# Splitting sixteen 8 KB SBUF buffers as four for weights and seven for gathered rows, instead of three and eight

## The chip, the cores and the metric

The kernel runs on one core of a Trainium2 chip. The metric is the device time of one execution in microseconds. The kernel before took 2333.25 us (median of 3 runs, 2330.32 to 2334.89). Below, a "piece" is a block of weights that one DMA brings into SBUF, a "row" is one gather of the last stage, and an "add" is the step that uses up a row.

## The reference, cut to what matters

One step of a one-layer streaming encoder, in float32, for 512 prompt frames and 32 frames of a second stream that has a cache of 512 past frames.

```
h = RMSNorm(x);  z = h @ w_in                 # q, k, v of two attentions, forget logits, gates
oA = DiffAttn(...), oB = FoX(...)             # 8 heads each
x = x + (sigmoid(gA)*(oA@w_pa) + sigmoid(gB)*(oB@w_pb)) @ w_o
q = RMSNorm(x) @ peer_wq                      # 1024 -> 2048
per frame and head: top 16 of 128 + 128 subkeys -> 16 experts of 16384
act = gelu(u[e] . x);  x = x + sum(softmax weight * act * v[e])   # 8 heads * 16 experts
y = RMSNorm(x)
```

For each frame 128 experts are fetched from a table whose line holds u (1024 floats) and v (1024 floats) of one expert, so 8 KB.

## The kernel before, in words

The 544 frames are five tiles: t = 0 to 3 of 128 frames, t = 4 of 32. A tile's work has two parts. Its *front* is attention (16 heads' steps, here called attend), norms and turns, the output projections, the product-key scores and the top-16 search (here called route). Its *experts* are 128 slots; slot s fetches, for each of the 128 frames (one per partition), the 8 KB line of that frame's expert. That is one row: a GpSimd indirect DMA of 1 MB (`gather`, line 677). For t = 4 each of the 32 frames takes four partitions, so there are 32 slots. In all 4 x 128 + 32 = 544 rows.

A row passes through three steps: VectorE takes the dot product of its u half with the frames (`dot`, L1618), ScalarE applies gelu to the 128 dot products (L941), and the v half is added, weighted. The add is done either by TensorE with a diagonal matrix (`add_v`, L1293, two matmuls of 512 columns) or by VectorE (L1643); a fixed table `ADDERS` says which. Slots are handled in pairs (HALF = 2), called half-blocks: both dots, then both weights or VectorE adds. TensorE runs the adds of a pair one step late, after the front piece that follows the pair (`held`, in the plan loop of TensorE).

All engines follow one list, `PLAN`, written by `make_plan`. It begins with the projection of tile 0 (27 chunks of w_in on 128 frames), then tile 0's front with the first chunks of the projection of tiles 1 to 4 between, and then, for t = 0 to 3, the pairs of experts of tile t with the front of tile t + 1 spread between them. For t = 0 the remaining projection chunks come first. The experts of t = 4 stand alone at the end. Each engine takes its part of the list in order, so a pair's dots wait behind the front piece ahead of them and the other way round.

Weights come in 159 pieces in the order of `WEIGHTS`: 52 chunks of w_in and 2 small ones, and for each front 4 of w_pa (1 MB), 4 of w_pb (0.5 MB), 4 of w_o, 8 of peer_wq and one of subkeys (1 MB each). w_pa and w_pb alternate. SyncE loads piece n into buffer n % WBUFS as soon as TensorE has finished piece n - WBUFS (`w_used`, raised at lines 1059, 1218, 1227, 1238, 1263, 1273):

```
if n >= WBUFS:
    sp.wait_ge(w_used, n - WBUFS + 1)
...
sp.dma_start(wb[:, 0:src.shape[1]], src).then_inc(landed, 16)
```

In the same queue stand the loads of q for the next tile, the saves of k and v, and the cache loads for the last tile.

Rows use slot s % RING. GpSimd issues row s when row s - RING has been dotted and added (line 677 in `gather`):

```
if s >= RING:
    who, count = ADDERS[s - RING]
    waits = [(dotted, s - RING + 1), (adders[who], count)]
gather(k, a, s % RING, waits)
```

Before the first row is fetched, the memory of the row buffers holds the inputs, h, and the front area of tile 0 (12,000 columns of each partition at most, of 16,384 with eight rows and 14,336 with seven).

Of the kernel before, what the change touches and what calls it, by code (L numbers as in the profile page):

```python
# [50 lines left out]
N_KEYS = 128  # L51
PC = 16
CW = 256
WBUFS = 3
RING = 8
BLOCK = 4
HALF = BLOCK // 2
DIAGS = 9
# [169 lines left out]
def landed_counts():  # L228

    count, out = [0] * WBUFS, []  # L230
    for n, _ in enumerate(WEIGHTS):
        count[n % WBUFS] += 16
        out.append(count[n % WBUFS])
    return out
# [112 lines left out]
def build(nc, d):  # L347
    with ExitStack() as ctx:  # L348
        def sb(name, shape, dt=F32):
            return ctx.enter_context(nc.sbuf_tensor(name, shape, dt))  # L350

        def sem(name):
            return ctx.enter_context(nc.semaphore(name))
# [4 lines left out]

        ring_all = sb("ring", [P, RING * 2 * D])
        ring = ring_all[:, :].rearrange("p (r n) -> p r n", r=RING)  # L360
        qT = sb("qT", [P, 12 * P])
# [3 lines left out]
        vb = sb("vb", [P, TILES, HEADS * DVB])  # L365
        wbuf = sb("wbuf", [P, WBUFS, KT, CW])
        bias = sb("bias", [P, HEADS, 2 * P])
# [21 lines left out]
        gw = sb("gw", [P, 2, SLOTS])  # L389
        dots = sb("dots", [P, RING])  # L390
        gel = sb("gel", [P, RING])
        gelw = sb("gelw", [P, RING])
        diag = sb("diag", [P, DIAGS, P])
# [47 lines left out]

        w_landed = [sem(f"w_landed{i}") for i in range(WBUFS)]
        w_used = sem("w_used")
# [65 lines left out]
        slot_free = sem("slot_free")  # L509
        row_landed = [sem(f"row_landed{r}") for r in range(RING)]  # L510
        seeded = sem("seeded")
# [82 lines left out]
        def _(sp):  # L594
# [11 lines left out]
            def save_kv():  # L606
                sp.wait_ge(z_stored, UNITS[len(GROUPS) - 1, CHUNKS])
                sp.dma_start(d["o_kaT"].rearrange("(k p) n -> p k n", p=P), kaT[:, :, :]).then_inc(kv_saved, 16)
                sp.dma_start(d["o_kbT"].rearrange("(k p) n -> p k n", p=P), kbT[:, :, :]).then_inc(kv_saved, 16)
                sp.dma_start(d["o_va"][0:SEQ, :].rearrange("(k p) n -> p k n", p=P), va[:, 0:4, :]).then_inc(kv_saved, 16)  # L610
                sp.dma_start(d["o_va"][SEQ:NTOK, :], va[0:DEC, 4, :]).then_inc(kv_saved, 16)
                sp.dma_start(d["o_vb"][0:SEQ, :].rearrange("(k p) n -> p k n", p=P), vb[:, 0:4, :]).then_inc(kv_saved, 16)
                sp.dma_start(d["o_vb"][SEQ:NTOK, :], vb[0:DEC, 4, :]).then_inc(kv_saved, 16)
# [12 lines left out]
            for n, (kind, piece) in enumerate(WEIGHTS):  # L626
                if n == last_z + 1:
                    save_kv()
                if n == WBUFS:
                    sp.dma_start(va[64:96, TILES - 1, :], d["norm2_g"].broadcast_to([32, D])).then_inc(rows_landed, 16)  # L630
# [1123 lines left out]
```

## Time and profile before

| | |
|---|---|
| median of 3 runs | 2333.25 us |
| profiled execution, device time | 2327.74 us |
| its span, first to last instruction | 2325.6 us |
| PE (matmul) busy | 1798.4 us, 77% |
| DVE busy | 1508.2 us, 65% |
| POOL busy | 757.1 us, 33% |
| ACT busy | 592.7 us, 25% |
| bytes moved by DMA | 765.01 MB, mean 329 GB/s |
| queue of the rows (q0) / of weights and SyncE (q1) | 570.46 MB / 169.48 MB |
| mean granted TensorE clock | 0.902 |

The span is the time between the first and the last instruction; the device time of the same execution is 2.1 us longer. PE, PEld, DVE, ACT and POOL are TensorE's matmuls, TensorE's weight loads, VectorE, ScalarE and GpSimd. "SPq" is SyncE's queue of DMA issues. Each group in the views of waits says for which instruction an engine stood idle and what ended the idle time.

### The profile page before, as it was taken

How to read it: one execution, taken by the hardware profiler on the slowest of the kernel's cores; microseconds unless marked ns; L12 is line 12 of the kernel's file. 1: busy time of each engine (PE TensorE's matmuls, PEld its weight loads, DVE VectorE, ACT ScalarE, POOL GpSimd, SP SyncE). 2: the span in 40 equal slices, each digit the busy share in tenths (PEclk: the TensorE clock that was granted, in tenths of full speed). 3: DMA queues.
4: the chain of work that ended last, by engine and by line, in shares of the span. 5: the costliest groups of instructions: out<-in, count | busy, mean ns of one | idle time of the engine just before them, and what ended most of it. 6: DMA issues, size and time to landing. Idle time of an engine off the chain costs nothing. (4 is left out here: it accounts for less than half of the span.)

```text
span 2325.6 us, 22972 instructions
## 1 busy us (share of the span) xinstructions
PE 1798.4 (77%) x7392; PEld 1085.4 (47%) x7392; DVE 1508.2 (65%) x3478; ACT 592.7 (25%) x1631; POOL 757.1 (33%) x697
## 2 busy tenths in 40 slices
PE   7988898789967776778787677878656787787755
PEld 6855774346635562334663233456422343563211
DVE  0021109576676459778667977785678788659966
ACT  3232011211143112344012234411222343013211
POOL 0000000454432023434334433342436344335443
PEclk9998999899997898888899889989998889999878
DMA  7832654999797787889999988899999879999987
GB/s 250 306 134 68 219 195 135 396 381 397 291 406 287 290 348 274 316 308 355 421 421 420 369 346 310 308 409 421 419 411 381 318 299 344 416 421 391 357 320 303
DMA packets 132071, 765.01 MB, mean 329 GB/s; under 512 B 19056, under 2 KB 34080, under 8 KB 44272
## 3 DMA queue, kind: packets, MB, share of 16 engines
q0 software_dynamic: 78336, 570.46, 61.8%
q1 hardware_dynamic: 30688, 169.48, 19.4%
q10 hardware_dynamic: 22928, 23.61, 2.9%
q8 instruction: 59, 0.97, 0.2%
q14 instruction: 60, 0.49, 0.1%
HBM read 744.77 MB, written 18.30 MB: 328 GB/s over the span
## 5 line engine op out<-in xcount | busy, mean ns | idle before, releaser
L677 POOL DMA_INDIRECT ring<-in_uv,stage x544 | 695.0, 1278 | 1122.8 <-PE acc L1293 452.8
L1293 PE MATMUL acc<-ring,diag 128*128 128x512 f32 (+1 forms) x1268 | 682.1, 687 | 225.3 <-ACT diag L953 133.0
L1618 DVE CUSTOM_DVE_ANT_0 ring<-ring,xb 128x1024 f32<-128x1024 f32 x544 | 646.1, 1220 | 115.1 <-DMA ring<-in_uv,stage 95.3
L1293 PEld LDWEIGHTS acc<-ring,diag 128*128 128x128 f32 (+1 forms) x1268 | 255.5, 213 | 604.6 <-issue 281.3
L941 ACT ACTIVATE gel<-dots 128x1 f32<-128x1 f32 x544 | 100.4, 199 | 880.7 <-DVE dots L1618 879.8
L1643 DVE SCALAR_TENSOR_TENSOR vsum<-ring,coefd,vsum 128x1024 f32<-128x1024 f32 x222 | 285.7, 1287 | 8.1 <-DVE coefd L1636 0.2
L1055 PE MATMUL pz<-F,wbuf 128*128 128x416 f32 (+1 forms) x656 | 244.4, 533 | 34.6 <-ACT F L814 29.8
L1055 PEld LDWEIGHTS pz<-F,wbuf 128*128 128x128 f32 (+1 forms) x656 | 127.1, 196 | 148.0 <-issue 148.0
L697 POOL COPY stage<-idx 128x4 int32<-128x4 int32 x136 | 59.3, 436 | 417.2 <-DVE gw L1574 399.0
L1636 DVE TENSOR_SCALAR coefd<-gel,gw 128x1 f32<-128x1 f32 x227 | 47.5, 209 | 160.8 <-ACT gel L941 160.4
L941 ACT ACT_TABLE_LOAD x67 | 86.0, 1283 | 36.8 <-issue 22.7
L1629 DVE TENSOR_SCALAR diag<-ident,gel,gw 128x128 f32<-128x128 f32 x159 | 55.1, 356 | 59.9 <-ACT gel L941 57.7
L1140 PE MATMUL pt<-ident,F 128*128 128x128 f32 (+2 forms) x224 | 35.1, 275 | 66.7 <-DVE F L1459 56.9
L1055 PE MATMUL pz<-wbuf,F 128*128 128x256 f32 (+1 forms) x384 | 85.0, 381 | 1.9 <-PE pz L1055 1.9
L1055 PE MATMUL pz<-ring,wbuf 128*128 128x128 f32 (+1 forms) x656 | 79.6, 281 | 6.8 <-ACT ring L778 3.4
L1055 PEld LDWEIGHTS pz<-ring,wbuf 128*128 128x128 f32 (+1 forms) x656 | 75.1, 191 | 14.0 <-issue 13.1
L1259 PE MATMUL pz<-F,wbuf 128*128 128x128 f32 x512 | 65.9, 291 | 15.5 <-DMA wbuf<-in_w_q 14.0
L1055 PEld LDWEIGHTS pz<-wbuf,F 128*128 128x128 f32 (+1 forms) x384 | 64.4, 170 | 22.7 <-issue 6.8
L1259 PEld LDWEIGHTS pz<-F,wbuf 128*128 128x128 f32 x512 | 63.1, 205 | 18.3 <-DMA wbuf<-in_w_q 15.7
L1259 PE MATMUL ps<-F,wbuf 128*128 128x128 f32 x512 | 62.5, 282 | 9.5 <-DMA wbuf<-in_w_q 7.7
L1259 PEld LDWEIGHTS ps<-F,wbuf 128*128 128x128 f32 x512 | 60.3, 197 | 13.5 <-DMA wbuf<-in_w_q 8.8
L1140 PEld LDWEIGHTS pt<-ident,F 128*128 128x128 f32 (+2 forms) x224 | 22.4, 143 | 90.8 <-DVE F L1459 72.2
(299 smaller groups left out, 2090.4 us busy)
## 6 DMA issues: line engine op xcount, KB each, us to landing
wbuf<-in_w_z SPq DMA_DIRECT2D x52, 1024.0 KB, 6.1
wbuf<-in_w_q SPq DMA_DIRECT2D x40, 1024.0 KB, 10.5
wbuf<-in_w_pa SPq DMA_DIRECT2D x20, 1024.0 KB, 10.8
wbuf<-in_w_o SPq DMA_DIRECT2D x20, 1024.0 KB, 10.0
wbuf<-in_w_pb SPq DMA_DIRECT2D x20, 512.0 KB, 9.2
ring<-in_uv,stage POOLq DMA_INDIRECT x544, 10.1
zt_mid<-F ACTq DMA_DIRECT2D x28, 192.0 KB, 5.1
wbuf<-in_w_sk SPq DMA_DIRECT2D x5, 1024.0 KB, 10.4
```

Source lines behind the costliest of these rows:

```text
L677: pool.indirect_dma_start(out=ring[:, slot, :], out_offset=None, in_=d["uv"], in_offset=bass.IndirectOffsetOnAxis(ap=stage[:, a, k:k + 1], ...
L697: nc.gpsimd.tensor_copy(stage[:, a, :], idx[:, t % 2, BLOCK * b:BLOCK * b + BLOCK]).then_inc(staged[a], 1)
L941: nc.scalar.activation(gel[:, slot:slot + 1], dots[:, slot:slot + 1], ACT.Gelu).then_inc(gelued, 1)
L1055: last = nc.tensor.matmul(out, left, right, start=(k == 0), stop=(k == KT - 1))
L1140: last = nc.tensor.transpose(pt[0:w, j * nq:(j + 1) * nq], p[0:nq, j * P:j * P + w], ident[0:nq, 0:nq])
L1259: last = nc.tensor.matmul(banks(t)[f % 4][:, 0:streamed(t)], w[:, k, j * P:(j + 1) * P], fa(t).xbT[:, k, 0:streamed(t)], start=(k == 0), s ...
L1293: last = nc.tensor.matmul(acc[0:nq, c * 512:(c + 1) * 512], diag[:, parity, 0:nq], ring[:, slot, D + c * 512:D + (c + 1) * 512], start=Fal ...
L1618: nc.vector.tensor_tensor_reduce(out=u, in0=u, in1=xb[:, t % 2, :], scale=1.0, scalar=0.0, op0=ALU.mult, op1=ALU.add, accum_out=dots[:, sl ...
L1629: nc.vector.tensor_scalar(diag[:, parity, 0:nq], pick[:, 0:nq], gel[:, slot:slot + 1], g, ALU.mult, ALU.mult).then_inc(coef_set, 1)
L1636: nc.vector.tensor_scalar(c, gel[:, slot:slot + 1], g, None, ALU.mult).then_inc(coefd_set, 1)
L1643: last = nc.vector.scalar_tensor_tensor(vsum[:, :], v, c, vsum[:, :], ALU.mult, ALU.add)
```

## The change

Two constants are changed. Everything that is derived from them follows: the buffer that a piece or a row uses, the piece or row that each issue waits for, the number of semaphores, and the place at which two small norm loads stand in SyncE's queue (after piece 4 and not piece 3).

```
-WBUFS = 3
-RING = 8
+WBUFS = 4
+RING = 7
```

One buffer for a piece is 8 KB of each partition, as is one for a row, so the SBUF in use stays the same but for three columns of small per-slot arrays.

## Rows read from the trace of the kernel before

**Rows 1.** The page, part 2: GB/s moved in 40 slices of 58.1 us.
```profile
GB/s 250 306 134 68 219 195 135 396 381 397 291 406 287 290 348 274 316 308 355 421 421 420 369 346 310 308 409 421 419 411 381 318 299 344 416 421 391 357 320 303
```

**Rows 2.** Busy time of each engine in stretches; last: granted clock, DMA share, GB/s.
```profile
core 0: us, PE busy (x) PEld busy (x) DVE busy (x) ACT busy (x) POOL busy (x), PEclk, DMA share, GB/s
743.00:801.00 58.00, 44.34 (x255) 39.88 (x256) 24.51 (x55) 1.98 (x9) 7.49 (x8) 0.87 0.89 359
801.00:855.00 54.00, 45.37 (x311) 39.13 (x309) 20.75 (x38) 12.00 (x32) 12.65 (x10) 0.91 0.80 322
945.00:1090.00 145.00, 111.86 (x379) 58.69 (x378) 111.91 (x233) 64.69 (x138) 55.85 (x56) 0.88 0.85 328
1118.00:1172.00 54.00, 40.35 (x227) 35.45 (x226) 35.88 (x72) 2.23 (x11) 15.51 (x15) 0.87 1.01 421
1653.00:1735.00 82.00, 47.66 (x97) 18.51 (x96) 57.58 (x215) 19.26 (x73) 30.64 (x30) 0.96 1.02 418
2033.00:2096.00 63.00, 51.76 (x324) 40.73 (x324) 35.86 (x64) 11.09 (x40) 21.59 (x19) 0.92 1.00 415
2096.00:2150.00 54.00, 42.30 (x94) 17.33 (x92) 53.36 (x200) 18.81 (x74) 29.94 (x28) 0.97 0.98 396
2224.00:2312.00 88.00, 49.65 (x80) 8.84 (x80) 62.53 (x115) 8.27 (x35) 41.38 (x39) 0.81 0.95 388
```

**Rows 3.** Waits in 743 to 860 us: engine, line, releaser, us in total, times, longest.
```profile
PE ps L1234 <- DMA wbuf<-in_w_o: 3.7, 1, 3.7
PE pz L1223 <- DMA wbuf<-in_w_pb: 3.1, 1, 3.1
PE pz L1214 <- DMA wbuf<-in_w_pa: 2.7, 1, 2.7
PE pz L1259 <- DMA wbuf<-in_w_q: 2.5, 1, 2.5
PE ps L1214 <- DMA wbuf<-in_w_pa: 1.5, 1, 1.5
PE ps L1259 <- DMA wbuf<-in_w_q: 0.7, 1, 0.7
```

**Rows 4.** The weight buffers over the whole span: idle us and times until a landing.
```profile
  DMA wbuf<-in_w_q: 46.2, 30
  DMA wbuf<-in_w_pa: 38.6, 17
  DMA wbuf<-in_w_o: 34.1, 18
  DMA wbuf<-in_w_pb: 23.2, 15
  DMA wbuf<-in_w_sk: 5.5, 4
```

**Rows 5.** Waits of VectorE for a row: 1090 to 1290, 1515 to 1735, 2224 to 2326 us.
```profile
DVE ring L1618 <- DMA ring<-in_uv,stage: 16.0, 11, 2.9
...
DVE ring L1618 <- DMA ring<-in_uv,stage: 35.0, 18, 3.7
...
DVE ring L1618 <- DMA ring<-in_uv,stage: 23.6, 22, 2.9
```

**Rows 6.** The timeline around row 161 (1047.94 its issue, 1059.36 its dot): start, us.
```profile
1047.94 2.00 POOL L677 DMA_INDIRECT ring<-in_uv,stage  x1 [0.30 <-issue]
1053.74 0.93 POOL L677 DMA_INDIRECT ring<-in_uv,stage  x1 [3.81 <-issue]
1059.36 1.22 DVE L1618 CUSTOM_DVE_ANT_0 ring<-ring,xb 128x1024 f32<-128x1024 f32 x1
```

**Rows 7.** Rows' time from issue to landing, 945 to 1090 us.
```profile
DMA to landing us min/median/max: 5.6/8.4/13.2
```

**Rows 8.** DMA issues 1118 to 1232 us: KB each, median us to landing.
```profile
wbuf<-in_w_q SPq DMA_DIRECT2D x8, 1024.0 KB, 11.4
ring<-in_uv,stage POOLq DMA_INDIRECT x28, 22.8
```

## The prediction

> **What bounds the kernel now.** I began with the page's slices of moved bytes [rows 1]. They stand at 409 to 421 GB/s in three blocks (slices 20 to 22, 27 to 30, 35 and 36) and lower elsewhere; no slice is above 421, so I take that as what this core's DMA gives. 1 MB (a row or a piece) then costs 1.048 / 421 = 2.5 us of DMA. The engines' busy time in stretches comes next [rows 2]. It tells four kinds of stretch apart: the weight part of a front with the DMA nearly but not quite full (743 to 855 us: share 0.89 and 0.80); the same part in later tiles with the DMA full (1118 to 1172 us: 1.01, 421 GB/s; 2033 to 2096 us: 1.00); attend, where no resource is full (945 to 1090 us: DMA 0.85, DVE 111.9 of 145 us); and the rows of the last tile, where the DMA is full again (2224 to 2312 us: 0.95 with its start). Then the waits. In the weight part of the first of these fronts TensorE waits for pieces, six waits of 14.2 us together [rows 3]. Over the whole span the weight buffers show 147.6 us of such waits [rows 4], but that view counts the weight load and its matmul, so about half, 74 us, is time. VectorE waits for rows 16.0, 35.0 and 23.6 us in the stretches with a full DMA [rows 5]; in the attend stretches the view of waits has none. So the bound changes: bytes in the full stretches, a chain across TensorE, VectorE and ScalarE in the others, with late pieces of weights in one of them.
>
> **The change part by part.** No instruction, no DMA and no byte is added or removed. Only the moment changes at which 159 pieces and 544 rows are issued.
>
> *Pieces, front of tile 1 (743 to 855 us).* The fourth buffer does two things. A fourth piece (the second of w_pb) is already there when the front begins, and a fourth of w_q is fetched while TensorE waits for the norm and the turn. The first removes the wait of 3.1 us on w_pb, the second those of 2.5 and 0.7 us on w_q [rows 3], 6.3 us in all. The three between (2.7, 1.5 and 3.7 us, 7.9 us) are waits on pieces in steady flow, with the DMA at 0.89: one more piece in flight brings them forward only as far as there is room. I take a third, 2.6 us. Sum 8.9 us off. Lower end 3.1 us (the first wait alone), upper end 14.2 us. TensorE sets the pace here (busy 44.3 of 58 and 45.4 of 54 us, VectorE 24.5 and 20.8 [rows 2]), and VectorE waits for no row, so what TensorE saves should be kept through the route stage.
>
> *Pieces, fronts of tiles 2 to 4.* What is left of the 74 us, about 60 us of waits, lies here. The DMA is full from before the weight part to well after it (421, 418 and 415 GB/s [rows 2]), and the engines work down one list in which pairs of rows and pieces alternate. In such a stretch the time to reach a point in the list is the bytes up to that point over 421 GB/s; a piece that comes sooner makes a row come later. I take 0 for tiles 2 and 3. In tile 4's front the rows are ahead of their dots, and VectorE is at its limit just behind (53.4 of 54 us at 2096 to 2150), so pieces that come sooner can start that stage sooner, until the DMA binds: of its 54 us it had 2% left, of the 63 before none. I take 2 us off. Ends for all three: 0, and 20 us each if the waits were plain stalls.
>
> A row shows how the two queues share a full DMA: between 1118 and 1232 us a row takes 22.8 us from issue to landing and a piece of w_q 11.4 us [rows 8], so a deep queue of rows does not hold the pieces back in proportion. The Trainium skill, "DMA: Bandwidth & Descriptors", section "Queues, rings and completion order", says that each DMA engine takes turns between the queues that have work, a packet at a time. By that rule a piece more in flight would not raise the weights' share while both queues have work, and the steady-flow third above (2.6 us) would be 0; by rows 3 I keep it.
>
> *Pieces, elsewhere.* In the first projection (0 to 135 us) and the first front (240 to 355 us) no wait for a piece over 0.5 us is in the view of waits, so 0; the front end could only lose if the fourth piece, issued at the start, crowded the small loads, and it stands behind them in the same queue. The copies and cache loads in SyncE's queue are each issued one piece sooner, behind waits of their own: 0.
>
> *Rows, attend stretches (945 to 1090, 1365 to 1515, 1800 to 1955 us).* With eight buffers row s waits for the add of row s - 8; for an odd s that is the odd row four pairs back. With seven it is the even row three pairs back: the odd row of each pair is issued about one pair later, the even row (released by the odd add just before it) as before. Row 161 shows the size [rows 6]. It was issued at 1047.94 us and dotted at 1059.36. Its new releaser is the add that now releases row 162, issued at 1053.74. So it goes from 11.4 us ahead to 5.6 us ahead, and the shortest landing in this stretch is 5.6 us, the median 8.4 [rows 7]. That row is just in time if it goes out into an empty DMA, which the later issue makes likelier (share 0.85), and 2.8 us late at the median. I read it as one of the tightest. VectorE has 33 us of idle time in these 145, so a late dot is partly absorbed. I take 1 us per stretch, 3 us on. Lower end 0; upper end: a quarter of the 68 pairs late by 2.8 us, 48 us.
>
> *Rows, entry to a full stretch and end of a tile.* Where the DMA becomes full (1100, 1515, 1965 us, and the last pairs of a tile), one row less has been fetched ahead, 2.5 us of DMA. There are three entries and three tile ends, 6 x 2.5 = 15 us if each time the DMA stood idle for want of that row. Between the attend share of 0.85 and the full 1.00 it was partly idle [rows 2], so I take a third, 5 us on. Lower end 0, upper 15.
>
> *Rows, last tile.* VectorE waits 22 times for a row there, 23.6 us [rows 5]: the bytes bind it (32 rows x 2.5 = 80 of 88 us). With one row less the queue is shorter but not empty: 0, upper end 5 us.
>
> **Sum.** 2325.6 - 8.9 - 2 + 3 + 5 = 2322.7 us of span, 2324.8 us with the 2.1 us around it. The profiled execution was 5.5 us under the median of the runs, so 2330.3 us there: 3 us or 0.12% faster, which is within what a measurement of this kernel can tell from no change (0.2%, 4.7 us).
>
> **The rivals.**
> 1. *The weight waits are worth more.* Then the first front gives all of its 14.2 us, and in tile 4 the fourth piece of w_q, fetched during the norm and the turn, starts the route stage sooner by the 2 x 2.5 = 5 us that a piece takes when it alternates with a row. 2333.25 - 14.2 - 5 + 5 = about 2319 us. For it: about 60 us of waits in later fronts, and in the last of these a VectorE at its limit just behind. Against it: DMA at 1.00 in all of them. It should show as fronts of tiles 2 to 4 that shorten while GB/s stays at 421.
> 2. *Seven rows are too few (slower).* The mechanism is the odd row of a pair in attend. VectorE does the dots in order, so a late odd row holds its add, the add holds the row three pairs on, and the loop closes over three pairs and not four. It decides once adds come later than (three pairs' time - landing of 8.4 us) after their dots. With 145 us for some 22 pairs (45 rows issued), 6.6 us each, that is 19.8 - 8.4 = 11.4 us, and an add by TensorE comes one step late: a pair's 6.6 us and its own pair's dots, gelu and diagonals behind the dot, so not far from it. If a third of the upper end (16 us) comes true and the entries cost 5, the time is 2333.25 - 8.9 - 2 + 16 + 5 = about 2343 us. For it: rows 6. Against it: VectorE waits for no row in attend now, so there is cover to lose first.
> 3. *The change does next to nothing*, for the fronts' gain stays with the first wait (3.1 us) and the rows lose nothing: 2330 us. It can't be told from the forecast by time, and counts with it.
>
> **How the numbers follow.** Forecast (with rival 3): 0.42; rival 1: 0.30; rival 2: 0.28. Forecast's own range 2326 to 2336 us. Of its 0.42, about 0.04 lies below the bound of 0.2% and 0.02 above it. So faster 0.34, same 0.36, slower 0.30. The range that holds 8 in 10 reaches into both rivals: 2318 to 2347 us.
>
> **What would show each step.** Right: no wait of TensorE on w_pb in the front of tile 1 and the q pieces without a wait; that front shorter by 6 to 12 us; at 421 GB/s the full stretches as long as before within 3 us; in attend a few waits of VectorE for rows, each under 3 us, together under 10 us. Wrong: fronts of tiles 2 to 4 shorter by 5 us or more each (rival 1), or waits for rows in attend of over 15 us with attend stretches longer than 145 to 155 us (rival 2). The prediction as a whole fails if the last row's dot comes over 5 us away from where it was, with tiles' spans not shifted as said.

## The result and the profile after

The changed kernel took 2338.55 us (median of 20 runs, 2331.03 to 2349.48) and the kernel before, run beside it, 2328.07 us (20 runs, 2319.63 to 2341.2). The ratio is 1.0045, interval 1.0031 to 1.0058: 10.5 us slower. The forecast was 0.12% faster; the time lies inside the range of 2318 to 2347 us, on the side that I had given 0.30. The profiled execution has a span of 2336.3 us, 10.7 us more than that of before, at a granted clock of 0.895 (before 0.902).

The page of the changed kernel: its span and part 2, GB/s in slices of 58.4 us. These answer to [rows 1]: still no slice above 421, and the three blocks near it are again slices 20 to 22, 27 to 30 and 35 and 36, the last two a little lower (391 to 421, and 414).

```profile
span 2336.3 us, 22973 instructions
...
GB/s 267 291 146 66 218 195 138 390 374 393 281 396 289 344 358 261 311 319 378 421 420 404 355 333 314 311 421 391 418 398 391 296 302 336 414 414 387 337 320 304
```

The table of stretches of the changed kernel answers to [rows 2], same columns (granted clock, DMA share and GB/s last). The stretches are chosen by eye for about the same work (TensorE's matmuls of the first two are 571 in the changed kernel, 566 in [rows 2]; the one at 2033 us holds 344 against 324 and is longer by that), so they show rates and not what was gained.

```profile
743.00:793.00 50.00, 40.72 (x247) 36.32 (x246) 22.68 (x51) 2.37 (x8) 10.33 (x10) 0.88 1.01 415
793.00:845.00 52.00, 45.84 (x324) 39.82 (x323) 23.65 (x44) 12.40 (x34) 10.84 (x10) 0.93 0.83 334
938.00:1083.00 145.00, 112.48 (x375) 58.75 (x376) 110.44 (x231) 64.49 (x137) 54.74 (x53) 0.87 0.83 321
1110.00:1164.00 54.00, 38.38 (x224) 33.78 (x223) 37.55 (x74) 2.43 (x12) 14.86 (x15) 0.84 1.01 421
...
1653.00:1735.00 82.00, 53.09 (x100) 20.46 (x99) 56.66 (x212) 19.36 (x73) 29.65 (x29) 0.90 1.02 418
2033.00:2099.00 66.00, 54.58 (x344) 41.05 (x342) 36.69 (x65) 11.42 (x41) 21.66 (x20) 0.95 1.01 418
2099.00:2156.00 57.00, 43.10 (x88) 17.31 (x88) 51.53 (x190) 18.20 (x72) 30.82 (x28) 0.94 0.97 382
2235.00:2323.00 88.00, 49.84 (x80) 8.98 (x80) 62.37 (x115) 8.38 (x35) 38.45 (x39) 0.81 0.94 388
```

The weight part of the first front is shorter, and its DMA went from 0.89 to 1.01 in the first half. The full stretches are full as before. Attend is unchanged (VectorE 110.4 of 145 us, before 111.9).

TensorE's waits for pieces in the first front, the changed kernel at 743 to 850 us, against the six of [rows 3] (engine, instruction, releaser, us in total, times, longest):

```profile
PE ps L1234 <- DMA wbuf<-in_w_o: 2.8, 1, 2.8
...
PE pz L1214 <- DMA wbuf<-in_w_pa: 1.1, 1, 1.1
...
PE pz L1234 <- DMA wbuf<-in_w_o: 0.7, 1, 0.7
```

14.2 us became 4.6. The waits on w_pb and on w_q are gone. Over the whole span the idle time in front of the weight buffers (us, times), against the 147.6 us of [rows 4], is 62.2 us:

```profile
  DMA wbuf<-in_w_pa: 33.7, 15
...
  DMA wbuf<-in_w_o: 13.4, 10
  DMA wbuf<-in_w_q: 9.6, 11
...
  DMA wbuf<-in_w_sk: 5.5, 4
```

What the weights gained, the rows lost. VectorE's waits for rows, the changed kernel at 938 to 1083, 1083 to 1285, 1513 to 1735 and 2235 to 2336 us, against none, 16.0, 35.0 and 23.6 us in [rows 5]. The first of them is not attend's: it is the wait of row 127's dot, the last of tile 0, which starts at 937.08 us and runs into the window.

```profile
DVE ring L1618 <- DMA ring<-in_uv,stage: 1.6, 1, 1.6
...
DVE ring L1618 <- DMA ring<-in_uv,stage: 39.4, 23, 3.8
...
DVE ring L1618 <- DMA ring<-in_uv,stage: 58.0, 32, 3.7
...
DVE ring L1618 <- DMA ring<-in_uv,stage: 23.6, 22, 2.5
```

The same over the whole span, from part 5 of the page (busy us, mean ns of one, idle before, its main releaser), first before, then after:

```profile
L1618 DVE CUSTOM_DVE_ANT_0 ring<-ring,xb 128x1024 f32<-128x1024 f32 x544 | 646.1, 1220 | 115.1 <-DMA ring<-in_uv,stage 95.3
```

```profile
L1618 DVE CUSTOM_DVE_ANT_0 ring<-ring,xb 128x1024 f32<-128x1024 f32 x544 | 649.1, 1221 | 188.6 <-DMA ring<-in_uv,stage 168.5
```

So 85 us less idle in front of weights (load and matmul both counted) and 73 us more in front of rows, while the time changed by 10 us. Neither figure by itself is time on the path: most waits were swapped for others.

Row 161, the row of [rows 6], in the changed kernel's timeline (start, duration, engine): issue, then dot.

```profile
1046.58 0.94 POOL L677 DMA_INDIRECT ring<-in_uv,stage  x1 [5.13 <-issue]
...
1052.19 1.22 DVE L1618 CUSTOM_DVE_ANT_0 ring<-ring,xb 128x1024 f32<-128x1024 f32 x1
```

It is issued 5.6 us ahead of its dot, as worked out, lands 0.1 us ahead of it, and no wait stands at the dot. Landing times in this stretch (938 to 1083 us) against [rows 7], and the issues at 1110 to 1220 us (KB each, median us to landing) against [rows 8]:

```profile
DMA to landing us min/median/max: 5.4/7.8/11.9
```

```profile
wbuf<-in_w_q SPq DMA_DIRECT2D x8, 1024.0 KB, 11.6
ring<-in_uv,stage POOLq DMA_INDIRECT x28, 21.4
```

A row now waits 21.4 us and not 22.8 in the full stretch, as there is one less of them; a piece takes 11.6 us, before 11.4.

**Where the time is.** To compare kernels I measured, in each timeline, from the start of one row's dot to that of another. Rows are numbered 0 to 543 over all tiles, so each stage holds the same work in every kernel. Two profiles of each of the first three kernels are given, since single stages differ by up to 3.4 us between two executions of the kernel before.

| stage (first to last row's dot), us | before | 3 and 7 buffers | 4 and 7 (changed) | 3 and 6 |
|---|---|---|---|---|
| weights of front 1 (82 to 100) | 118.4, 115.0 | 113.8, 114.2 | 107.9, 107.7 | 113.7 |
| weights of fronts 2 to 4 (178 to 206, 306 to 334, 438 to 464), sum | 348.6, 348.0 | 349.6, 350.8 | 346.4, 344.5 | 353.0 |
| route, tiles 1 to 3 (206 to 246, 334 to 374, 464 to 502), sum | 349.5, 352.5 | 355.5, 355.9 | 356.6, 354.1 | 380.2 |
| ends of tiles, the last ten rows and what follows up to attend (118 to 136, 246 to 264, 374 to 392, 502 to 512), sum | 204.3, 201.1 | 215.0, 217.0 | 215.7, 211.7 | 225.1 |
| attend (136 to 170, 264 to 298, 392 to 430), sum | 341.1, 340.2 | 338.6, 340.2 | 339.8, 338.5 | 353.4 |
| turn after attend (170 to 178, 298 to 306, 430 to 438), sum | 60.1, 60.1 | 64.3, 64.1 | 66.2, 66.2 | 69.4 |
| last tile (512 to 543) | 80.0, 80.2 | 79.8, 79.9 | 79.5, 79.8 | 81.9 |

Means against before: ends +11.0, turns +6.1, routes +4.4, attend -1.5, weights of fronts 2 to 4 -2.8, of front 1 -8.9. Sum +8.3 us, of the 10.5 timed. The spans of these profiles differ by 12.2 us in the mean, and 3.5 of that lies ahead of row 82, where executions scatter most: that row's dot starts at 727.2 and 725.1 us in before and at 728.1 and 731.2 us in the changed kernel, and the wait for rows is not longer there by more than 2 us.

### The profile page after: what moved, and what is told of

Read it like the earlier page. It is cut to its first block and busy times, and to the rows that moved or that the text cites. A ratio compares the mean times of both kernels' runs of the same rounds, so it can differ in the third digit from the quotient of the medians.

```text
span 2336.3 us, 22973 instructions
## 1 busy us (share of the span) xinstructions
PE 1805.9 (77%) x7392; PEld 1083.4 (46%) x7392; DVE 1510.6 (65%) x3478; ACT 593.7 (25%) x1631; POOL 738.8 (32%) x697
## 5 line engine op out<-in xcount | busy, mean ns | idle before, releaser
L677 POOL DMA_INDIRECT ring<-in_uv,stage x544 | 675.7, 1242 | 1150.6 <-issue 362.0
L1293 PE MATMUL acc<-ring,diag 128*128 128x512 f32 (+1 forms) x1268 | 698.7, 701 | 239.9 <-ACT diag L953 139.1
L1293 PEld LDWEIGHTS acc<-ring,diag 128*128 128x128 f32 (+1 forms) x1268 | 261.9, 218 | 629.6 <-issue 290.1
L941 ACT ACT_TABLE_LOAD x67 | 86.0, 1283 | 36.7 <-issue 22.7
L1259 PE MATMUL pz<-F,wbuf 128*128 128x128 f32 x512 | 61.0, 278 | 6.2 <-DMA wbuf<-in_w_q 2.9
L1259 PEld LDWEIGHTS pz<-F,wbuf 128*128 128x128 f32 x512 | 58.4, 192 | 8.9 <-issue 5.0
## 6 DMA issues: line engine op xcount, KB each, us to landing
wbuf<-in_w_q SPq DMA_DIRECT2D x40, 1024.0 KB, 10.7
wbuf<-in_w_o SPq DMA_DIRECT2D x20, 1024.0 KB, 14.7
```

Of the source, the lines that this page charges most:

```text
L677: pool.indirect_dma_start(out=ring[:, slot, :], out_offset=None, in_=d["uv"], in_offset=bass.IndirectOffsetOnAxis(ap=stage[:, a, k:k + 1], ...
L941: nc.scalar.activation(gel[:, slot:slot + 1], dots[:, slot:slot + 1], ACT.Gelu).then_inc(gelued, 1)
L1259: last = nc.tensor.matmul(banks(t)[f % 4][:, 0:streamed(t)], w[:, k, j * P:(j + 1) * P], fa(t).xbT[:, k, 0:streamed(t)], start=(k == 0), s ...
L1293: last = nc.tensor.matmul(acc[0:nq, c * 512:(c + 1) * 512], diag[:, parity, 0:nq], ring[:, slot, D + c * 512:D + (c + 1) * 512], start=Fal ...
```

## The experiments

**One part alone: seven rows, three pieces**, and **one row fewer still**.

```
-RING = 8
+RING = 7        (second kernel: RING = 6)
```

> Three buffers for pieces as before, seven row buffers: the row part of the change alone. Theory A (the trace after: the loss is one row less fetched ahead where the DMA is full and at the ends of the tiles, 20 us, and the pieces give 10 us back): about 18 to 22 us slower than before, ratio 1.008 to 1.010; waits of VectorE for rows well over the 95 us of before; attend stretches as long as before. Rival B (the fourth piece takes DMA from the rows, and seven rows alone cost little): within 5 us of before.

> Three buffers for pieces, six row buffers. If what is lost is bytes fetched ahead (one row, 2.5 us, at some eight places), six rows lose about twice what seven lose: some 40 us, ratio 1.017. If it is the loop of an odd row that closes over three pairs where it closed over four, six rows close over three pairs too, for both rows of a pair, and lose little more than seven: 20 to 28 us, ratio 1.009 to 1.012.

Measured: 2348.52 us with seven rows (before 2328.63), ratio 1.0086, interval 1.0069 to 1.0103, so +20 us, as theory A had it. With six 2407.59 us, ratio 1.0335, interval 1.0317 to 1.0353: +79 us, where neither theory had over 40. VectorE's line for the dots in part 5, first seven rows, then six:

```profile
L1618 DVE CUSTOM_DVE_ANT_0 ring<-ring,xb 128x1024 f32<-128x1024 f32 x544 | 648.4, 1220 | 156.5 <-DMA ring<-in_uv,stage 137.1
```

```profile
L1618 DVE CUSTOM_DVE_ANT_0 ring<-ring,xb 128x1024 f32<-128x1024 f32 x544 | 652.1, 1221 | 249.3 <-DMA ring<-in_uv,stage 231.8
```

The first buffer taken away costs 20 us and the second 59 us more. In the table above the ends (+13.3, then +22.4 us) and the turns (+4.1, +9.3) go about in proportion to the number of rows missing. Routes (+4.7, +29) and attend (-1.3, +12.7) don't: the second row costs there many times what the first did. (Numbers are means over the profiles of a kernel, where there are two.) VectorE's waits for rows lie in the same places: in the ends 8.8 and 8.5 us in the two profiles of before, 18.9 and 20.8 with seven rows, 31.0 with six; in the routes 32.9 and 33.1, then 40.9 and 40.6, then 68.3; in attend 0, then 1.0 and 1.2, then 28.7. This points to two mechanisms, of which the second is hardly paid for at seven rows. That it is the loop from a row's add to the landing of the row six on is my reading; no run shows it by itself, and with six rows there is one profile.

**Are the full stretches bound by bytes?** The first three pieces of the next front (pa, pb, pa: 2.5 MB) are fetched in the route stage, when the DMA is full, and lie unused through attend. One wait in SyncE's queue keeps them back for fronts 2 to 4 until all rows of the tile before are added (`summed`), which falls into the stretch called an end here. It is done to both kernels.

```
 if n >= WBUFS:
     sp.wait_ge(w_used, n - WBUFS + 1)
+if (kind, piece) == ("pa", 0) and fronts >= 2:
+    sp.wait_ge(summed, fronts - 1)
```

> The kernel before (3 and 8) with one wait more in SyncE's queue: the first pieces of the next front are not fetched behind the subkeys but only once the tile before is summed, for the fronts of tiles 2, 3 and 4. That takes 2.5 MB, 6.2 us of DMA, out of each of the full stretches and puts it into attend, where the DMA has room. If bytes bind those stretches, as I said: 8 to 18 us faster, ratio 0.992 to 0.997. If the rows' latency or VectorE binds the route stage there, 0 to 4 us.

> The changed kernel (4 and 7) with the same wait. The pieces held back are four, 3.5 MB or 8.7 us of DMA each time. If bytes bind: 12 to 22 us faster than the changed kernel, so 2 to 12 us faster than before. If the rows' latency binds since there are seven buffers, it stays within 5 us of the changed kernel (ratio to before 1.002 to 1.006).

Measured: the kernel before with the wait 2316.21 us, ratio 0.9941 (0.9918 to 0.9964), 13.7 us faster by the ratio; the changed kernel with it 2324.4 us, ratio to before 0.9987 (0.9969 to 1.0005), so 0.58% or 13.5 us under the changed kernel. (There four pieces are held back, pa, pb, pa, pb, which is 3 MB or 7.5 us and not the 3.5 MB or 8.7 us of the expectation.) SyncE's timeline of the first, around the place (the pieces after w_sk went out from 1220.55 us on in the kernel before):

```profile
1217.37 0.33 SPq L640 DMA_DIRECT2D wbuf<-in_w_sk  x1
...
1365.65 0.33 SPq L640 DMA_DIRECT2D wbuf<-in_w_pa  x1
1366.02 0.43 SPq L640 DMA_DIRECT2D wbuf<-in_w_pb  x1
```

And its windows at two tile ends (columns as in [rows 2]), to be held against the ends shown below:

```profile
1333.00:1388.00 55.00, 39.14 (x85) 15.65 (x86) 41.16 (x83) 16.69 (x41) 21.55 (x22) 0.88 1.01 411
1768.00:1823.00 55.00, 34.01 (x64) 12.76 (x64) 41.91 (x81) 9.61 (x25) 27.17 (x26) 0.83 1.01 414
```

The DMA is now at 1.01 in these ends, which carry 2.5 MB more each, and the two together take 113.8 us, in the two profiles of before 113.8 and 110.9. The gain is in the routes of tiles 1 and 2: 113.6 us against 117.2 and 118.0, and 124.0 against 131.7 and 130.5, together 11 us, where 2.5 MB / 421 = 6.2 us each is what the bytes say. In the changed kernel the same two routes lose 6.5 and 6.1 us of the 7.5 by bytes. In tile 0's route, where the DMA was idle for 21 of 81 us before, holding the pieces gives nothing (81.6 us). So the full stretches are bound by bytes, in both kernels, and a piece moved out of one is worth nearly its bytes. The ends of tiles 1 and 2 are not: they took in 2.5 MB more each and were no longer than in before's first profile.

**The pieces' part alone.** Four buffers and eight rows together find no room in SBUF, so this was not tried in that form. Instead a fourth place was made, for pieces of fronts 1 to 4 only, out of the q buffer widened from 1536 to 2048 columns; the 2 KB per partition for it come from DIAGS = 5 in place of 9. It can be used only from the end of a tile's attend on, so unlike the changed kernel's fourth buffer it holds nothing through attend. The core of the edit:

```
-DIAGS = 9
+DIAGS = 5
-qT = sb("qT", [P, 12 * P])
+qT = sb("qT", [P, KT * CW])
...
-if n >= WBUFS:
-    sp.wait_ge(w_used, n - WBUFS + 1)
+if BEFORE[n] >= 0:                        # last piece in the same place
+    sp.wait_ge(w_used, BEFORE[n] + 1)
+if PLACES[n] == WBUFS and BEFORE[n] < last_sk:
+    sp.wait_ge(scored, 24 * (fronts + 1)) # q of this tile has been used
```

> Eight row buffers and three for pieces, and a fourth place for pieces that costs no row buffer: from the end of a tile's attend to its subkeys q lies unused, and its memory (made 512 columns wider; the diagonals of the adds have five buffers and not nine for it) takes every fourth piece in the fronts of tiles 1 to 4. It is the piece part of the change without the row part. If the two parts add up (changed kernel = row part + piece part), it is 8 to 12 us faster than before, ratio 0.995 to 0.997. If the piece part helps only because fewer rows compete, it is within 4 us of before.

Its control, DIAGS = 5 alone:

> The kernel before with five buffers for diagonals where it has nine, the control for the run before this one: within 3 us of before, since an add is at most two pairs behind its diagonal.

Measured: 2312.08 us, ratio 0.9941 (0.992 to 0.9962); the control 2325.03 us, ratio 0.9992 (0.9972 to 1.0012). The pieces' part is then 0.9941 / 0.9992 = 0.9949, 12 us faster. From the other side, the changed kernel over the one with seven rows and three pieces is 1.0045 / 1.0086 = 0.9959, 9.5 us faster. By the intervals the first can be off by some 7 us and the second by 5, so they agree, and both are clear of zero. TensorE's waits for pieces in the first front (738 to 862 us) of the kernel with the part-time buffer, same columns as above:

```profile
PE ps L1262 <- DMA wbuf<-in_w_o: 2.8, 1, 2.8
PE ps L1242 <- DMA wbuf<-in_w_pa: 2.5, 1, 2.5
PE pz L1242 <- DMA wbuf<-in_w_pa: 1.1, 1, 1.1
PE pz L1262 <- DMA wbuf<-in_w_o: 0.6, 1, 0.6
```

**Both things that paid**, the part-time fourth place and the wait, with eight rows:

> Both: the fourth place in q's memory with eight row buffers, and the first pieces of the next front held back until the tile before is summed. The wait alone gave 12 to 14 us; the fourth place should give 8 to 12 more: 2306 to 2312 us where before is at 2329, ratio 0.990 to 0.993. Any less and the two draw on the same time.

Measured: 2306.82 us, ratio 0.9913 (0.9892 to 0.9933), 20 us under the kernel before and the fastest here. The two gains apart, 13.7 us each by their ratios, would add up to 27.5, 7 us more than the 20. Each of the three ratios is uncertain by 5 us, so the 7 us are not clear of noise, and that the two draw on the same time is not shown. The profiles speak against it: from row 82's dot to the end of the span they take 1595.8 us in the mean of before, 1583.8 with the wait, 1577.0 with the place and 1562.8 with both, so there the gains of 12.0 and 18.8 us add up (33.0). What is missing lies ahead, mostly before the first row, where neither edit changes what is issued: that row was issued at 416.6 us with both, at 403.3 and 408.1 in before, 413.6 and 407.1 with one. What made that head longer is open.

**A second profile of three kernels**, to know how far a stage's length can be trusted:

> The kernel before once more, for a second profile of it. What differs between the two profiles of one kernel, stretch by stretch, is the size under which a difference to the changed kernel says nothing: I expect up to 5 us by the start of the rows and in the front of tile 1, under 2 us in each later stretch.

> The changed kernel once more, for a second profile. If the loss sits where the first profile has it, the stretches from the last route pairs of a tile to the third pair of the next are again 3 to 4 us longer than in both profiles of before (55 us at the end of tile 0, 56 at tile 2), the attend stretches are not, and the share of idle DMA grows by what the stretch grows. If the rows are held by a full DMA and not by the seven buffers, the idle DMA stays.

> Three and seven once more, for the same stretches: ends of tiles together 8 to 14 us longer than before with as much more idle DMA, turns 2 to 5 us, attend within 2 us each. The front of tile 1 tells the second thing: 113 to 116 us there (first profile 113.8, before 115.0 and 118.4) would mean that seven rows cost nothing in that front and that the fourth piece alone makes it 108.

Measured, one execution each: before 2320.47 us; changed 2334.21 and seven rows with three pieces 2355.8 us, both beside 2326.56 us for before. The stages are in the table. The second profile of before is 7 us shorter, 3.4 of it in the weights of front 1, and single later stages differ by as much (the end of tile 1 took 58.0 and 54.8 us, the last route 100.6 and 104.0), more than the 2 us that I expected, so a single difference under 3.5 us says nothing. The sums of the ends, of the turns and of the routes are larger with seven rows than with eight in every pair of profiles. One thing expected did not come: in the second profile of the changed kernel the end of tile 0 took 55.2 us, as in before.

## Why the prediction was wrong, step by step

**Pieces, front of tile 1: right in size, with one part of three not shown.** Foretold -8.9 us; the stage is 8.9 us shorter than the mean of before. That the two agree to a tenth is luck: the kernel with the wait and the control, which do here what before does, took 112.7 and 114.2 us, and against the mean of all four the gain is 7.3. The wait on w_pb went, as said, and that on w_q all but 1.1 us in the second profile. Those in steady flow were to give a third of their 7.9 us. In the kernel with the part-time place and eight rows they still add up to 7.0 us (2.8, 2.5, 1.1, 0.6), and in the changed kernel's two profiles they are 4.6 and 7.1. With three pieces they are 7.9 and 7.5 in before, but 6.2 with the wait, 4.2 and 4.6 with seven rows and 4.3 in the control, so no gain on them is shown. Against seven rows and the control the stage shortens by 6.2 us (seven rows; the changed kernel against them) and 6.8 (the control; the part-time place against it), about the 6.3 of the first two parts. The rule of the Trainium skill that was weighed there ("DMA: Bandwidth & Descriptors", "Queues, rings and completion order"), by which this part would be 0, is nearer to these rows than my third.

**Pieces, fronts of tiles 2 to 4: right, the last too small.** Foretold 0, 0 and -2 us. Against seven rows and three pieces, the changed kernel's weight part of front 4 is 4.8 us shorter (112.0 and 112.1 against 116.3 and 117.3), the other two within what repeats differ by (115.3 and 115.9 against 115.9 and 117.1; 119.1 and 116.5 against 117.4 and 116.4). The 60 us of waits there were nearly all time that the DMA needed anyway. With eight rows the same part is 110.7 us with the part-time place, 116.5 and 116.2 in before and 115.0 in the control. Of rival 1 the part in front 4 came true (5 us there), the rest did not: front 1 gave 7 to 9 us and not 14.2. Pieces together: foretold -10.9, measured -9.5 to -12 us.

**Rows, attend: too dear.** Foretold +3 us, measured -1.5, which is within what repeats differ by. In the stretch of [rows 6] no dot of attend waits for a row, and in all three attends together they wait 2.2 and 1.6 us. Rival 2's loop of three pairs, which I had named as the way to be slower, is not what made it slower: attend is no longer with seven rows. It does begin to bind with six (+12.7 us).

**Rows, entry to a full stretch and end of a tile: this step failed.** I had the right mechanism, one row less fetched ahead, with a price of 2.5 us a place, and then took a third of 6 x 2.5 = 15 us because the DMA is "partly idle" between attend and the full stretch. Measured with seven rows alone: four ends +13.3 and three turns +4.1 us, which is 17.4 / 7 = 2.5 us a place, the full price in the mean; and routes, for which I had no term, +4.7. That is 22 us where 5 stood. VectorE's waits for rows grew by about as much there (ends +11.2, turns +4.7, routes +7.8), which ties the loss to rows that land late. Only the mean is 2.5 us: single ends grew by 1.7 to 5.9 us, two of the turns by 0.6 and 0.7 and the third by 2.9, and which places count was settled after the result. The ends of the kernel before (second profile), then with seven rows and three pieces, then changed; tiles 0 to 2, columns as in [rows 2]:

```profile
921.00:976.00 55.00, 38.48 (x89) 16.25 (x89) 40.47 (x81) 19.45 (x43) 20.60 (x21) 0.84 0.79 309
1335.00:1390.00 55.00, 37.45 (x93) 15.24 (x92) 42.49 (x81) 16.21 (x37) 22.71 (x23) 0.91 0.90 365
1770.00:1826.00 56.00, 36.07 (x77) 14.03 (x76) 42.25 (x81) 9.46 (x26) 24.71 (x25) 0.85 0.91 368
```

```profile
923.00:981.00 58.00, 40.74 (x89) 17.12 (x89) 40.47 (x81) 19.45 (x43) 22.41 (x20) 0.82 0.77 292
1343.50:1400.30 56.80, 40.05 (x96) 16.50 (x95) 42.51 (x81) 16.34 (x37) 22.69 (x24) 0.88 0.86 344
1783.00:1846.00 63.00, 39.10 (x78) 15.16 (x77) 42.94 (x81) 9.57 (x28) 25.71 (x25) 0.79 0.85 344
```

```profile
917.00:975.00 58.00, 40.90 (x89) 17.21 (x89) 40.57 (x82) 19.45 (x43) 22.27 (x20) 0.82 0.77 295
1337.00:1396.00 59.00, 43.44 (x96) 17.45 (x94) 42.36 (x80) 16.13 (x37) 22.79 (x23) 0.83 0.85 336
1780.00:1839.00 59.00, 33.33 (x72) 13.02 (x72) 41.81 (x80) 8.82 (x25) 24.00 (x24) 0.84 0.88 361
```

VectorE is busy for the same 40.5 and 42.4 us, to 0.1, in the first two ends of all three. The DMA share falls: in the end of tile 1 from 0.90 to 0.86 and 0.85. Idle DMA, (1.01 - share) times length, summed over the four ends, is 37.1 and 36.7 us in the two profiles of before, 44.8 and 44.1 with seven rows, and 44.0 and 40.5 in the changed kernel. So with seven rows 7.5 of the 13.3 us are idle DMA, and most of the rest is bytes: 68.4 MB came in the ends, against 66.0 in before, which is 5.7 us at 421 GB/s, nearly all of it in the ends of tiles 2 and 3. They had not been fetched ahead. I had read idle DMA as spare room that would hide the loss. It is room for other traffic, as the pieces held back show, but not for rows, which had no free buffer to go to. At the end of a tile the front piece between the pairs is gone, and the last ten dots come 2.0 to 2.1 us apart in the mean in before, faster than the 2.5 us in which the DMA brings a row; in the changed kernel they come 2.2 to 2.5 us apart. What was fetched before lets VectorE run ahead, and the DMA can only fetch ahead into a free buffer. In the route before it the DMA stands idle for want of a free buffer: row 118 of the changed kernel landed at 895.18 us and was dotted at 916.77, so its buffer was taken for 21 us with data that waited. Routes of tiles 1 to 3 have 13 and 16 us of idle DMA in the two profiles of before and 21 in both with seven rows, worked out in the same way. One buffer fewer is one row fewer in store.

The end of tile 0 shows it row by row. The kernel before: dot of row 118, issue of row 125, dot of row 125.

```profile
926.76 1.22 DVE L1618 CUSTOM_DVE_ANT_0 ring<-ring,xb 128x1024 f32<-128x1024 f32 x1
...
927.42 1.37 POOL L677 DMA_INDIRECT ring<-in_uv,stage  x1 [1.46 <-issue]
...
941.44 1.22 DVE L1618 CUSTOM_DVE_ANT_0 ring<-ring,xb 128x1024 f32<-128x1024 f32 x1
```

The changed kernel: dot of row 118, issue of row 125 (now behind row 118's add), its dot, and the dot of row 127.

```profile
916.77 1.23 DVE L1618 CUSTOM_DVE_ANT_0 ring<-ring,xb 128x1024 f32<-128x1024 f32 x1
...
924.70 1.71 POOL L677 DMA_INDIRECT ring<-in_uv,stage  x1 [5.87 <-DVE dots L1618]
...
931.45 1.22 DVE L1618 CUSTOM_DVE_ANT_0 ring<-ring,xb 128x1024 f32<-128x1024 f32 x1
...
937.08 1.23 DVE L1618 CUSTOM_DVE_ANT_0 ring<-ring,xb 128x1024 f32<-128x1024 f32 x1 [1.55 <-DMA ring<-in_uv,stage]
```

Counted from row 118's dot, row 125 goes out after 0.7 us in one and after 7.9 us in the other, and both times its dot comes 14.7 us after. It landed 8.0 us ahead of its dot in before and 0.2 us ahead in the changed kernel; for row 126 that is 3.3 and 0.3 us, for row 127 1.4 and 0. (The profile puts row 125's late issue down to a dot that ended at 924.46 us; TensorE's last matmul of row 118's add ended at 923.90.) Rows 118 to 127 take 18.7 us in before and 20.3 in the changed kernel. That the dot of row 127 waits, for 1.5 to 2.0 us, is so in four of the five profiles with seven rows and in none with eight; in the changed kernel's second profile it does not, row 125 lands 3.0 us ahead, and the end is no longer than before's.

A rival that I did not test is the clock. The granted clock in the ends is lower in some of them too (0.91 in tile 1's of before, 0.88 and 0.83 in the others), and a slower TensorE adds later and so frees buffers later. The lines above show the second profile of before; in the first, at 0.85, this end took 58.0 us with eight rows. Whole executions are not ordered by it: the two profiles with seven rows and three pieces have 0.903, against 0.902 and 0.901 in before, and spans of 2344.0 and 2353.7 us. At an equal clock the ends of tiles 2 and 3 are still longer with seven rows (tile 2 at 0.84 to 0.85: 59.8 and 59.8 against 55.8, 56.1 and 56.5 us; tile 3 at 0.88 to 0.89: 38.5 against 35.4, 35.4, 35.5 and 35.7), that of tile 1 hardly (at 0.88: 56.7, 58.3 and 59.3 against 56.9). So part of the 13.3 us may go with the clock; whether it adds to the loss or follows from it, no run tells. And whether an end loses by the shorter store or by the loop from add to landing (row 125: 7.4 us from the end of that add to its landing), these runs don't part: seven rows shorten both.

**Rows, last tile: right.** Foretold 0, measured 0.4 us less; 22 waits of 23.6 us, the same as in [rows 5].

**The sum.** Pieces -10.9 foretold and -9.5 to -12 measured; rows +8 foretold and +20 measured. The miss of 12 us is this one term, made smaller by what attend did not cost. The price of 2.5 us a place was right in the mean (17.4 us over seven places); the third taken of it was wrong, a seventh place and the routes were missed.

## What to carry to other kernels

When buffers move from one stream to another, price each stream at the places where it lives on stock: a spell of demand faster than the DMA, behind a spell in which the DMA was idle because the buffers were full. There a buffer was worth, in the mean, its full transfer time each time the spell came; idle DMA at such a place is a sign that the stock is short, and it is room for other traffic alone. Before buying a buffer, see what lies in those that are there: moving the fetch of three pieces, which came in a full stretch and lay unused through the next, was worth as much (13.7 us) as a whole buffer (9.5 to 12 us). This is what the Trainium skill, "Perfetto Trace Analysis", section "Optimization Strategy", says of kernels with several regimes, that interleaving the regimes may pay; the run agrees, with 0.59%.

## What the runs showed of the hardware that I had not expected

The cost of taking away row buffers rises steeply: 20 us for the eighth, 59 us for the seventh, while the bytes and the instructions stay the same, and VectorE's waits for rows grow from 95.3 to 137.1 and 231.8 us.

The idle share of the DMA rose together with the waits for it: the end of tile 1 at 0.90 with eight buffers and 0.85 to 0.86 with seven, while VectorE waits more for rows. And one kernel's stages repeat less well than its total suggests: the weights of front 1 took 118.4 and 115.0 us in two executions of the same program, the end of tile 0 58.2 and 55.2 us in two of the changed one.
